# Scale tiles as the standing operand of TensorE, the two conditioning columns moving, and five smaller edits

## The reference

```python
mod = silu(c) @ w_mod + b_mod            # for c_ctx and for c
sh1, sc1, g1, sh2, sc2, g2 = jnp.split(mod, 6, axis=-1)
h = x * (1 + sc1) + sh1
out, finals = mixer(h, l, p, init, fourier_fn)   # mLSTM (4 heads) and a Fourier branch
x = layer_norm(ALPHA * x + g1 * out, ...)
h2 = x * (1 + sc2) + sh2
a, u = jnp.split(h2 @ p['w_ffn_in'][l], 2, axis=-1)
f = (jax.nn.silu(a) * u) @ p['w_ffn_out'][l]
x = layer_norm(ALPHA * x + g2 * f, ...)
```

## Time and profile before

| | us |
|---|---|
| median of 3 runs | 1384.67 |
| the profiled execution | 1384.84 |
| its span, first to last instruction | 1382.7 |
| TensorE matmul busy | 1361.7 (98%) |
| VectorE busy | 860.4 (62%) |
| GpSimd busy | 747.3 (54%) |
| ScalarE busy | 467.1 (34%) |

### The profile page before, as it was taken

One profiled execution on the slowest core, in us unless ns is written; L12 is line 12 of the kernel. 1 busy time (PEld: TensorE's weight loads), 2 busy tenths in 40 slices (PEclk: granted clock), 3 DMA queues, 4 the chain that ended last, 5 costly groups with the idle time before them and its releaser, 6 DMA issues.

```text
span 1382.7 us, 23138 instructions
## 1 busy us (share of the span) xinstructions
PE 1361.7 (98%) x8693; PEld 1294.0 (94%) x8693; DVE 860.4 (62%) x1458; ACT 467.1 (34%) x828; POOL 747.3 (54%) x417
## 2 busy tenths in 40 slices
PE   9999999999999999999999999989999999999997
PEld 5999999899899989999999999988999999988886
DVE  6875984357426724753587376487877777764307
ACT  4834321231222122221324100266554455463220
POOL 0274775632462354145335666455988889852440
PEclk9999999999999999999999999999999999999999
DMA  9633643211412231142027555613222212242321
GB/s 382 226 108 137 214 149 133 79 64 55 142 68 67 94 109 46 65 145 76 30 91 237 190 183 187 170 64 137 92 91 91 91 62 89 92 168 76 122 77 76
DMA packets 59563, 165.07 MB, mean 119 GB/s; under 512 B 8152, under 2 KB 22624, under 8 KB 58216
## 3 DMA queue, kind: packets, MB, share of 16 engines
q1 hardware_dynamic: 38712, 143.53, 30.3%
q10 hardware_dynamic: 20784, 20.69, 4.7%
HBM read 146.86 MB, written 17.34 MB: 119 GB/s over the span
## 4 chain that ended last, share of the span: by engine, by line
PE 67%; DVE 11%; issue 8%; POOL 6%; DMA 4%; ACT 3%; SPq 0%; DVEq 0%; ACTq 0%; POOLq 0%
PE psum L1425 19%; PE psum L998 15%; PE psum L1462 11%; PE psum L1315 8%; PE psum L1297 3%; PE psum L1063 3%; POOL w_hi L820 3%; POOL w_lo L824 2%; DVE nt_a L2406 2%; PE psum L1169 2%; PE psum L1253 2%; DMA raw<-in_wunits 2%; PE psum L1055 1%; DVE yl L2448 1%; PE psum L1027 1%
## 5 line engine op out<-in xcount | busy, mean ns | idle before, releaser
L820 POOL TENSOR_TENSOR w_hi<-raw,zero 128x1024 fp32r<-128x1024 f32 x78 | 152.3, 1952 | 346.7 <-PE psum L998 280.9
L824 POOL TENSOR_TENSOR w_lo<-raw,w_hi 128x1024 fp32r<-128x1024 f32 (+1 forms) x111 | 268.8, 2422 | 130.6 <-ACT w_hi L2111 73.5
L1425 PE MATMUL psum<-t_r,ws_r 128*128 128x322 f32 x1848 | 276.6, 311 | 2.0 <-POOL ws_r L898 0.7
L1425 PEld LDWEIGHTS psum<-t_r,ws_r 128*128 128x128 f32 x1848 | 275.0, 189 | 3.2 <-issue 2.0
L998 PE MATMUL psum<-h_hi,w_hi 128*128 128x256 f32 (+1 forms) x768 | 176.2, 310 | 1.1 <-PEq L1361 1.0
L998 PE MATMUL psum<-h_lo,w_hi 128*128 128x256 f32 (+1 forms) x768 | 174.9, 309 | 0.0
L998 PE MATMUL psum<-h_hi,w_lo 128*128 128x256 f32 (+1 forms) x768 | 174.8, 309 | 0.0
L898 POOL TENSOR_TENSOR ws_r<-ws_f,ws_r 128x512 fp32r<-128x512 f32 x88 | 124.1, 1410 | 33.7 <-DVE ws_f L2675 20.9
L998 PEld LDWEIGHTS psum<-h_hi,w_hi 128*128 128x128 f32 x768 | 137.8, 188 | 2.4 <-issue 1.7
L998 PEld LDWEIGHTS psum<-h_lo,w_hi 128*128 128x128 f32 x768 | 139.8, 188 | 0.0
L998 PEld LDWEIGHTS psum<-h_hi,w_lo 128*128 128x128 f32 x768 | 139.7, 188 | 0.0
(11 more groups left out here) (359 smaller groups left out, 3070.3 us busy)
## 6 DMA issues: line engine op xcount, KB each, us to landing
raw<-in_wunits SPq DMA_DIRECT2D x124, 512.0 KB, 3.4
pair<-in_wunits SPq DMA_DIRECT2D x46, 512.0 KB, 4.3
mod_slot<-in_wmod SPq DMA_DIRECT2D x16, 512.0 KB, 14.5
mod_ring<-in_wmod ACTq DMA_DIRECT2D x16, 512.0 KB, 3.5
yg_dram<-yg_sb ACTq DMA_DIRECT2D x20, 256.0 KB, 3.0
yg_st<-yg_dram SPq DMA_DIRECT2D x16, 320.0 KB, 3.8
c_raw<-in_stateC SPq DMA_DIRECT2D x4, 1028.0 KB, 6.6
z_ring<-in_wmod SPq DMA_DIRECT2D x8, 512.0 KB, 4.4
```

What stands on the lines that cost most here:

```text
L820: pool.tensor_tensor(hi, src, zero[:, 0:1].broadcast_to([P, src.shape[1]]), ALU.add)\
L824: pool.tensor_tensor(lo, src, hi.bitcast(F32), ALU.subtract).then_inc(w_split, 1)
L1425: ins = mm(out, ws_r[n][:, w, cols], t_r[:, n, k, x, :], start=(starts and k == 0 and m == 0), stop=(k == HALF_K - 1 and m == 2), skip_gro ...
```

## The change

1. In the front the roles of `scale_part` are swapped: of each scale tile eight blocks of 128 x 128 stand in turn, and the two columns of `c_silu` move. The result comes in columns, so the turn and the copies to `sc_rows` go.
2. The 1 MB load of `silu_z` goes. TensorE makes it from `c_silu`: 16 products of a column broadcast as the standing operand with the identity moving, into banks 2, 3, 6 and 7; ScalarE copies both halves out, between its first folds. 20 of the 44 idle matmuls go. The scale tiles' loads stand between the pairs of token rows. TensorE's order is now parts 0 to 2, positions 0 and 1, parts 3 to 5, position 2, and so on. VectorE takes shift tile 0 ahead of the even rests.
3. GpSimd splits unit 4 before it waits for the gate weights.
4. `gated(h, 3)` moves into the middle of `combine(h, 4)`; it stood behind it and behind `qk_rest(h + 1, 1)`.
5. g2 is transposed on TensorE between the merge and the output projection, copied by ScalarE and stored with one DMA of 16 rows of 512 B. Its load back is two DMAs in pieces of 512 B.
6. Two semaphores are counted anew (`stats_done` shares the one of the broadcast); this moves nothing.

```diff
@@ -141,7 +141,7 @@
         x1_dram = nc.dram_tensor("x1_dram", [P, KD, NT], F32, kind="Internal").ap()
-        g2_dram = nc.dram_tensor("g2_dram", [2, KD, P], F32, kind="Internal").ap()
+        g2_dram = nc.dram_tensor("g2_dram", [KD, 2, P], F32, kind="Internal").ap()
@@ -170,7 +170,7 @@
         silu_row = mod_sum
-        sc_rows = at("sc_rows", [2, UW], F32, [em_at[0] - 8 * UW])
+        g2_t = silu_row[0:2 * KD, 0, 0:P]
         sc_f = at("sc_f", [P, KD, 2], F32, [em_at[0] - 4 * UW])
@@ -514,14 +515,16 @@
                                           (fold_lo_ok, 6), (table_hi_ok, 4), (table_ok, 4))]
-        ws_sum_ok = {P5: Again(gate_act, 5), P6: Again(gates_ok, 2), P7: Again(sc_rows_ok, 2), P3: Again(mod_done, 9)}
+        ws_sum_ok = {P5: Again(gate_act, 5), P6: Again(gates_ok, 2), P7: Again(sc_rows_ok, 0), P3: Again(mod_done, 8)}
         held_ok = [Again(s, n) for s, n in ((zero_ok, 2), (gate_acc, 1), (em_acc, 1))]
...
         c_read, u_read = Again(bmod_ok, 1), Again(once, 2)
-        g2_stored, g2_in = Again(xf_in[2], 32), Again(xf_in[2], 64)
+        g2_stored, g2_in = Again(xf_in[2], 32), Again(xf_in[2], 48)
+        g2_turned, g2_copied = Again(em_ok, 2), Again(v_ones, 2)
         scaled_ok = Again(norm_ok, 0)
...
+        spread_ps = [flat[:, a * 512:(a + 2) * 512] for a in (2, 6)]
         silu_ps = flat[:, 4 * 512:8 * 512].rearrange("p (g c) -> p g c", g=2)
@@ -580,7 +583,7 @@
         N_SMALL = 5
-        N_IDLE = 44
+        N_IDLE = 24
         X_PARTS = (slice(0, 2), slice(2, 5), slice(5, KD))
@@ -624,9 +627,8 @@
                 sp.dma_start(x_par[:, i, :], x_fold[1, i]).then_inc(xf_in[i], 16)
-            scale_in(0, 1)
-            sp.dma_start(silu_z[:], c_rows).then_inc(row_in, 16)
-            scale_in(2, 3)
+                scale_in(i)
+            scale_in(3)
             shift_in(0)
@@ -783,9 +785,10 @@
             sp.wait_ge(f_f_ok, KF)
-            sp.wait_ge(g2_stored.sem, g2_stored.base + 32)
-            sp.dma_start(g2_row[:], g2_dram.rearrange("g k p -> g (k p)").unsqueeze(0).broadcast_to([P, 2, DMODEL]))\
-                .then_inc(g2_in.sem, 16)
+            sp.wait_ge(g2_stored.sem, g2_stored.base + 16)
+            for g in range(2):
+                sp.dma_start(g2_row[:, g, :].rearrange("q (k p) -> q k p", p=P),
+                             g2_dram[:, g, :].unsqueeze(0).broadcast_to([P, KD, P])).then_inc(g2_in.sem, 16)
             for m in range(4, 2 * NU):
@@ -843,9 +846,10 @@
             unit(3)
+            unit(4)
             pool.wait_ge(gate_act, 1)
             pool.tensor_tensor(gw_lo[:], gate_w[:], gw_hi[:].bitcast(F32), ALU.subtract).then_inc(gates_ok, 1)
-            for u in range(4, U_B):
+            for u in range(5, U_B):
                 unit(u)
@@ -1023,18 +1027,9 @@
                 pe.wait_ge(mod_in[n], 16)
-                for half in range(2):
-                    ins = mm(psum[0:2, half, :], c_silu[:, n, :], slots[n][:, half * 512:(half + 1) * 512],
-                             start=(n == 0), stop=(n == KD - 1))
-                ins.then_inc(mod_done, 1)
-
-            def scale_columns():
-
-                pe.wait_ge(const_in, 16)
-                for n in range(KD):
-                    if n % (KD // 2) == 0:
-                        pe.wait_ge(sc_rows_ok, 2)
-                    ins = pe.transpose(psum[:, 0, 2 * n:2 * n + 2], sc_rows[:, n * P:(n + 1) * P], ident[0:2, 0:2])
+                for f in range(KD):
+                    ins = mm(psum[:, 0, 2 * f:2 * f + 2], slots[n][:, f * P:(f + 1) * P], c_silu[:, n, :],
+                             start=(n == 0 and f == 0), stop=(n == KD - 1 and f == KD - 1), skip_group_check=True)
                 ins.then_inc(mod_done, 1)
@@ -1070,6 +1065,12 @@
             pe.wait_ge(once, 1)
+            pe.wait_ge(const_in, 16)
+            for g in range(2):
+                for k in range(KD):
+                    ins = mm(spread_ps[g][:, k * P:(k + 1) * P], c_silu[:, k, g:g + 1].broadcast_to([P, P]), ident,
+                             start=True, stop=True)
+                ins.then_inc(row_spread, 1)
@@ -1103,17 +1104,17 @@
-            for n in range(2):
+            for n in range(3):
                 scale_part(n)
...
                 position(i)
-            for n in range(2, 6):
+            for n in range(3, 6):
                 scale_part(n)
+            pe.wait_ge(row_ok, 2)
             position(2)
...
             position(3)
-            scale_columns()
             for i in range(4, 2 * KD):
@@ -1370,6 +1371,9 @@
                     unit_cols(joined(p), U_MIX + 2 * j + q, q, yg_hi[q], yg_lo[q], first=(q == 0), last=(q == 1))
+            pe.wait_ge(mod_sum1, 5 * KD)
+            pe.transpose(psum[0:2 * KD, 4, 0:P], mod_sb[:, 5 * KD:6 * KD, :].rearrange("p k g -> p (k g)"), ident)\
+                .then_inc(g2_turned.sem, 1)
@@ -1526,12 +1530,12 @@
                 A_(xo_hi[:, i, :], xo_f[:, i, :], ACT.Copy).then_inc(fold_hi_ok, 1)
+                if i < 2:
+                    act.wait_ge(row_spread, i + 1)
+                    A_(silu_z[:, i, :], spread_ps[i], ACT.Copy).then_inc(row_ok, 1)
             for i in range(KT):
...
                 A_(xe_hi[:, i, :], x_rep[:, i, :], ACT.Copy).then_inc(fold_hi_ok, 1)
-            act.wait_ge(row_in, 16)
-            for g in range(2):
-                A_(silu_z[:, g, :], silu_z[:, g, :], ACT.Silu).then_inc(row_ok, 1)
             act.wait_ge(const_in, 16)
@@ -1556,9 +1560,6 @@
             act.wait_ge(mod_done, KD)
-            for half in range(2):
-                A_(sc_rows[:, half * 512:(half + 1) * 512], psum[0:2, half, :], ACT.Copy).then_inc(sc_rows_ok, 1)
-            act.wait_ge(mod_done, KD + 1)
             A_(sc_f[:].rearrange("p a b -> p (a b)"), psum[:, 0, 0:2 * KD], ACT.Copy).then_inc(sc_ok, 1)
@@ -1879,7 +1880,7 @@
             gate_a(7)
-            act.wait_ge(row_in, 32)
+            act.wait_ge(row_in, 16)
             act.wait_ge(st_dve, 2 * H + 2)
@@ -1900,10 +1901,10 @@
-            act.wait_ge(mod_sum1, 5 * KD)
-            for g in range(2):
-                act.dma_start(g2_dram[g].rearrange("k p -> p k"), mod_sb[:, 5 * KD:6 * KD, g],
-                              allow_slow_non_contiguous=True).then_inc(g2_stored.sem, 16)
+            act.wait_ge(g2_turned.sem, g2_turned.base + 1)
+            A_(g2_t, psum[0:2 * KD, 4, 0:P], ACT.Copy).then_inc(g2_copied.sem, 1)
+            act.wait_ge(g2_copied.sem, g2_copied.base + 1)
+            act.dma_start(g2_dram.rearrange("k g p -> (k g) p"), g2_t).then_inc(g2_stored.sem, 16)
             act.wait_ge(aug_f_ok, 1)
@@ -2193,7 +2194,9 @@
                 v.tensor_tensor(x_rep[:, i, :], x_rep[:, i, :], x_par[:, i, :], ALU.add).then_inc(fold_ok, 1)
-            for i in range(KT):
+
+            def even_rest(i):
+
                 v.wait_ge(fold_hi_ok, KT + i + 1)
@@ -2223,7 +2226,10 @@
-            for k in range(4):
+            shift_tile(0)
+            for i in range(KT):
+                even_rest(i)
+            for k in range(1, 4):
                 shift_tile(k)
@@ -2541,10 +2547,9 @@
                 gated(h, 2)
-                combine(h, 4, chain)
+                combine(h, 4, chain, 3)
                 if not last:
                     qk_rest(h + 1, 1)
-                gated(h, 3)
                 if not last:
@@ -2830,7 +2835,7 @@
             v.wait_ge(rows2_ok, KD + 2)
-            v.wait_ge(g2_in.sem, g2_in.base + 16)
+            v.wait_ge(g2_in.sem, g2_in.base + 32)
             for tt in range(TT):
```

More of the change, by code:

```diff
@@ L398, in build @@
         row_ok = sem("row_ok")
+        row_spread = sem("row_spread")
         zero_ok = sem("zero_ok")
@@ L483, in build @@
         s2_ok = sem("s2_ok")
-        stats_done = sem("stats_done")
+        stats_done = Again(row_spread, 2)
         stats_seen = sem("stats_seen")
@@ L1381, in column_sums @@
                         ins = mm(out[:, a:z], ones_r[:].bitcast(F32), total[:, a:z], start=True, stop=True)
-                ins.then_inc(stats_done, 1)
+                ins.then_inc(stats_done.sem, 1)
             pe.wait_ge(taken[0], A_OUT + 1)
@@ L2029, in _ @@
             hold(2, 0, 0, True)
-            act.wait_ge(stats_done, 1)
+            act.wait_ge(stats_done.sem, stats_done.base + 1)
             A_(musq[:], sums_ps[0], ACT.Square, scale=1.0 / DMODEL).then_inc(mu_ok, 1)
```

## The result

The changed kernel takes 1418.11 us (median of 6, 1410.02 to 1424.11) against 1384.57 for the kernel before; the ratio is 1.0239, with an interval from 1.0208 to 1.0271. The forecast was 1377, in a range of 1375 to 1389. The executions of the kernel before lie within 2.8, those of the changed one within 14: something in it varies from one to the next.

What follows compares the result with a forecast made beforehand. TensorE, busy 98% of the span, was taken as the bound. Front -1.4, GpSimd's order -1.3, heads -1.9 and g2 -3.2 summed to -7.8 from 1384.84, giving 1377, in a range of 1375 to 1389.

Steps and rivals of the forecast that it cites:

- GpSimd's order: Unit 4 split before the gate weights' wait: TensorE's wait of 1.27 goes, -1.3, or 0 if unit 4's weights land late.
- g2: Output projection: without the scattered stores weights arrive earlier and waits at units 3 and 4 shrink; -3.2, between -2 and -3.6.
- -1.4: Front: TensorE gains at most 1.4 before `side` waits for `e_lo`; 0 if broadcasts or row pairs come 2 later.
- rival B: Front: TensorE's clock falls while parts mostly load weights, +9 to +13; total 1386 to 1392, say 1389; chance 0.22.
- rival A: Heads: head 0 misses through the store's long landing, +3 instead of -1.9; all else holds, total 1382; chance 0.25.
- the prediction's 1392: Upper end of the total given for the clock falling in the front, +9 to +13 with -7.8 or -2.9.
- Scale parts: Front: 16 load-and-matmul pairs a tile at 0.11, 14.1 in all, no gain; bounds -5 and +10; the turn goes, -0.6.
- The bound in VectorE's `e_lo`: Front, `side`: VectorE's eighth `e_lo` block is ready at 51.7, so TensorE gains at most 0.6 + 0.8 = 1.4.
- When the parts start: Front: idle matmuls end at 10.5 to 11, broadcasts take 3.6 and end at about 14.3, scale tile 2 lands at 17.9.
- The heads: Moving `gated(h, 3)` removes `turn`'s wait of 0.7 in three heads; head 3 gets +0.2; -1.9 in all.
- the short landing: Heads: the store of `gated(h, 2)` lands in 4.0 to 4.3, not 5.9, so no wait and -0.7 a head.

Runs made afterwards that it cites:

- order_g2: Kernel before with only GpSimd's order (unit 4 ahead of the gate weights' rest) and g2's transpose and store of rows: 1381.17 us, ratio 0.9979.
- after_off0: Changed kernel with TensorE's loop over the heads placed at slot 0 of a block of 256 instructions: 1400.28 us, ratio 1.0100.
- order_g2_gated: Kernel before with GpSimd's order, g2's transpose and the gating of tile 3 moved as in the change: 1393.57 us, ratio 1.0055.
- slots 128 and 205: Kernel before with only TensorE's loop over the heads placed at slot 128 or 205 of a block of 256 instructions: 1391.75 and 1389.89 us.
- before_off252: Kernel before with only TensorE's loop over the heads placed at slot 252 of a block of 256 instructions: 1402.89 us, ratio 1.0134.

## Why the prediction was wrong

The loss of 33.5, by medians of one edit each (the two steps at 1400.3 lean on four executions that lie 15 apart and are rough; the +18.0 at slot 252 is a steady figure):

| step | us | forecast |
|---|---|---|
| front without the swap, GpSimd's order, g2 (1384.9 to 1380.2) | -4.7 | -5.9 |
| the scale tiles standing (1380.2 to 1392.9) | +12.6 | part of -1.4; rival B, +9 to +13 |
| the gating moved (1392.9 to 1400.3; +12.4 alone) | +7.4 | -1.9; rival A, +3 |
| the loop's place (1400.3 to 1418.1; +18.0 alone at slot 252) | +17.8 | not named |

Three steps failed: a term that the prediction put at nothing (the code), a branch that it took the wrong way (the clock in the front), and a wait that it took to be short (the store in the heads). Its rivals do not reach the result either: A and B together, -2.9 and +9 to +13, make 1391 to 1395 (the prediction's 1392 is a slip), and the rest is the code.

**The step that is missing** is the code. I priced each added instruction by its duration and never by its place in the program; loading it again was put at nothing, without a reason, and costs 17.8 to 18.0. I had counted loads and matmuls in the front. That their number moves the loop of 1691 instructions from 7 blocks to 8, and its start to the end of a block, stands in no row that I showed. One stood on the page: 37 packets, for a program of 37 to 38 blocks. So the loop was executed four times and loaded once. (The slot of the changed kernel's loop itself is not read anywhere. That one product is issued between its two stops puts it within some ten instructions of a block's end, and 199 less is then a slot between 47 and 56, from which 1691 instructions fit in 7 blocks.) A body in 7 blocks stays (37 or 38 packets; the kernel before branches back over it without a stop), one in 8 doesn't (64 or 65 packets), and no run shows why.

**Scale parts: the wrong case was taken.** The pairs came at 0.11 at the high clock and at 0.21 at the low one, as forecast (0.11, and twice that). The views give the clock as a share, 1.00 and 0.50. The prediction's 2.4 and 1.2 GHz are an estimate from its idle matmuls, 512 columns divided by 0.21 and by 0.43, as if a column took a cycle; no view shows a clock in GHz. Rival B had the mechanism, its price (+9.7 at `side`, +12.6 by medians, against +9 to +13) and its places. The mistake was its chance, 0.22, and that the forecast's -1.4 took the clock to stay. What spoke against it was only that the trace "has no fall in its short stretches of transposes", which says nothing of 14 us. The bound in VectorE's `e_lo` was not reached, as TensorE came later than VectorE.

**When the parts start.** Near enough: idle matmuls to 9.4 (10.5 to 11), broadcasts 3.6 long (3.6), tile 2 at 17.9 (17.9). The -1.4 of the front is nowhere reached: even with the tiles moving, `side` starts 1.0 earlier.

**GpSimd's order.** The wait went as said, but I asked what is late next for the weights alone. `uf_lo` took 0.5 of it: from `side` to the turn of `em_rows` the changed kernel and the one with moving tiles gain 0.7 (1.3), and order_g2, in its one trace, nothing.

**The heads.** "I take the short landing" failed. Rival A had the right chain to the end: two instructions of GpSimd sat out, a wait of 5 (5.7 measured). Seen standing under GpSimd are `nt_a` (1.91 and 2.19 against 0.22) and `hn_sb` (2.51 against 0.55); that it holds for all of VectorE's two-operand instructions on SBUF is not shown. Wrong were where and how often. I tied the long landing to head 0, from one execution. In the changed kernel's trace TensorE waits 2.3 in head 0 and 0.5 in heads 2 and 3; in after_off0's it waits 5.7 in head 2 and 4.7 in head 3, for which I had said +0.2; in the short execution of order_g2_gated it waits in none. And behind the long waits the clock is down (0.59 in after_off0's 616:620), another 1.8, which I had not priced. Landings of 4.0 to 6.3 in one execution were the range of a variable, not four constants, and what they go with stood in the same trace: the state's load, which lands 0.7 to 0.9 before the store in heads 0 to 2.

**g2.** Right. In the changed kernel the output projection begins 35.8 late and the feed-forward part 32.5: -3.3 (-3.2). ScalarE's timeline there, where the earlier trace rows waited 3.16 for its weights:

```profile
929.28 1.06 ACT L1928 ACTIVATE w_hi<-raw 128x1024 fp32r<-128x1024 f32 x1 [1.15 <-PE psum L1002]
```

It waits for TensorE alone and starts 35.8 behind 893.5, as forecast. The wait at unit 3 is gone, and of the 1.25 at unit 4 there are 0.46 left (0.3 forecast):

```profile
943.70 0.57 PE L1002 MATMUL psum<-mg_hi,w_hi 128*128 128x256 f32 x2 [0.46 <-POOL w_lo L827]
```

**What stays open.** Why a reload costs 5 to 7.5 at slots 128 and 205, and whether slot 101 is the exact edge; neither was tried further. That the state's load holds up `yg_sb`'s store is read from 42 pairs that land together; no run moved the load away. Why the load itself takes 5.6 or 8.3 is open, and so is why the clock is low for longer in some executions of the front.

## What to carry over

Where TensorE runs a large real loop (here 1691 instructions), count them and find its slot before pricing an edit ahead of it: here some 200 instructions more reloaded code at each turn (65 packets against 37, 17.8), and one aligning line took that away. Pairs of a 128-column load and 2 columns cost TensorE its clock here, for the positions between and behind them too (12.6 in all); moving 64 columns under the same loads gave 12.3 back. A wait moved into a chain of small instructions costs what the chain then meets (here GpSimd's splits, 12.4 in the median), so put it behind the chain's result. And when a wait is for a transfer, look at what other transfers are under way at that moment before taking its shortest time (here 3.9 to 6.6 beside the state's load).

## What the runs showed of the hardware that was not expected

- TensorE's loop of 1691 instructions runs without reloads where it lies in 7 blocks of 256, by the estimate above (37 or 38 packets), and reloads at each turn in 8 (64 or 65). The price for three turns and the exit is 18.0 with 4 instructions of the body in the first block, and 5 and 7.5, not to be told apart, with 51 and 128.
- After a stop of 3.8 to 4.3 (before_off252) or of 4.7 or 5.7 (after_off0), or two of 1.5 to 1.9 and 2.0 to 2.5 (the changed kernel), a window of 4 us reads half the clock or little more (0.50 to 0.63). Of six single stops of 1.3 to 1.9 at the borders (slots 128 and 205) one, of 1.9, had a fall behind it (0.72).
- A 256 KB store from ScalarE's queue, issued 2.0 to 2.5 behind a 1 MB load from SP's queue, landed 0.7 to 0.9 behind it in 42 cases of 42, after 3.9 to 6.6.
- Moving 64 columns behind each 128-column load, where 2 are needed, had no price that the time shows (1380.6, against 1380.2 with the tiles moving), and in parts 3 to 7 the clock read 1.00 from 28 on with 64, and 0.50 to 0.72 with 2.
